# Two chained transformer blocks on one core: three projections token tile by token tile, and one operand stored interleaved

## What is computed

```python
def hybrid_layer(x, c, ...):
    ...
    merged = gates[:, :, 0] * (br_a @ wa) + gates[:, :, 1] * (br_b @ wb) + gates[:, :, 2] * (br_c @ wc)
    y = merged @ w_out
    x = x + gate_m[:, None] * rmsnorm(y, g_mix_post)
    h2 = rmsnorm(x, g_ff_pre) * (1.0 + scale_f[:, None]) + shift_f[:, None]
    y2 = jnp.square(jax.nn.relu(h2 @ w_ff1)) @ w_ff2
    return x + gate_f[:, None] * rmsnorm(y2, g_ff_post)

def second_block(x, mem, ...):
    ...
        x = x + rms_norm(y, post_mix_g[l])
        h = rms_norm(x, pre_x_g[l])
        m = rms_norm(mem, mem_g[l])
        x = x + rms_norm(memory_cross_attention(h, m, w_xq[l], w_xkv[l], w_xo[l]), post_x_g[l])
        h = rms_norm(x, pre_ffn_g[l])
        f = jnp.square(jax.nn.relu(h @ w_ff1[l])) @ w_ff2[l]
        x = x + rms_norm(f, post_ffn_g[l])
```

## Time and profile before

| | us |
|---|---|
| median of 3 runs (lowest, highest) | 831.03 (830.16, 831.48) |
| the profiled execution | 831.31 |
| its span, first to last instruction | 830.1 |
| PE busy | 797.3 |
| DVE, ACT, POOL busy | 566.9, 430.9, 85.6 |
| mean granted TensorE clock | 0.992 |

### The profile page before, as it was taken

How to read it: one execution, slowest core, us unless ns; L and a number is a source line. 1 busy time by engine, 2 the same in 40 slices (tenths; PEclk the granted TensorE clock), 3 DMA queues, 4 the chain that set the end, 5 groups by cost and what they waited for, 6 DMA issues and landing times.

```text
span 830.1 us, 12160 instructions
## 1 busy us (share of the span) xinstructions
PE 797.3 (96%) x4852; PEld 701.6 (85%) x4852; DVE 566.9 (68%) x759; ACT 430.9 (52%) x640; POOL 85.6 (10%) x129
## 2 busy tenths in 40 slices
PE   3999999999989999999999999999999999999995
PEld 2889988999879888888889998788987988888884
DVE  4886987879955575665567889847556566655563
ACT  4445256663446564545456477547545644454441
POOL 6301970001110000000001000011000100000000
PEclk9999999999998999999999999999999999999998
DMA  9978977776644655656656554445434566656641
GB/s 305 363 237 276 356 254 254 280 251 231 227 128 153 195 184 180 195 173 189 200 180 199 176 159 153 151 156 201 154 102 126 156 199 185 196 185 195 183 149 51
DMA packets 83319, 163.64 MB, mean 197 GB/s; under 512 B 5424, under 2 KB 13808, under 8 KB 83264
## 3 DMA queue, kind: packets, MB, share of 16 engines
q1 hardware_dynamic: 81344, 157.31, 58.3%
q10 hardware_dynamic: 1424, 4.81, 1.7%
q0 software_dynamic: 496, 0.76, 0.3%
HBM read 161.81 MB, written 1.05 MB: 196 GB/s over the span
## 4 chain that ended last, share of the span: by engine, by line
PE 83%; DVE 7%; ACT 5%; issue 2%; POOL 1%; DMA 1%; SPq 0%; ACTq 0%; DVEq 0%; POOLq 0%
PE bank L1664 19%; PE bank L1666 18%; PE bank L1665 18%; PE bank L1692 13%; PE bank L1694 6%; DVE ada_acc L924 2%; DVE lo_ring L892 2%; PE bank L1854 1%; ACT hi_ring L472 1%; PE bank L2188 1%; PE bank L2209 1%; DVE x_residual L997 1%; DMA ada_ring<-in_w_ada 1%; PE bank L1723 1%; ACT gates L527 1%
## 5 line engine op out<-in xcount | busy, mean ns | idle before, releaser
L892 DVE TENSOR_TENSOR lo_ring<-raw_ring,hi_ring 128x1024 fp32r<-128x1024 f32 x248 | 306.7, 1240 | 172.6 <-ACT hi_ring L472 172.1
L472 ACT CAST hi_ring<-raw_ring 128x1024 fp32r<-128x1024 f32 x248 | 258.8, 1050 | 272.6 <-PE bank L1666 181.9
L1664 PE MATMUL bank<-h_hi_lo,hi_ring 128*128 128x256 f32 x560 | 164.7, 294 | 4.3 <-DVE lo_ring L892 1.9
L1665 PE MATMUL bank<-h_hi_lo,hi_ring 128*128 128x256 f32 x560 | 159.0, 284 | 0.0
L1666 PE MATMUL bank<-h_hi_lo,lo_ring 128*128 128x256 f32 x560 | 158.9, 284 | 0.0
L1692 PE MATMUL bank<-h_hi_lo,hi_ring 128*128 128x512 f32 x448 | 158.7, 398 | 0.0
L1664 PE MATMUL bank<-hi_ring,branch_hi 128*128 128x512 f32 x320 | 126.6, 395 | 0.0
L1694 PE MATMUL bank<-h_hi_lo,lo_ring 128*128 128x256 f32 x448 | 125.8, 281 | 0.0
L1666 PE MATMUL bank<-hi_ring,branch_lo 128*128 128x512 f32 x320 | 124.8, 390 | 0.0
L1665 PE MATMUL bank<-lo_ring,branch_hi 128*128 128x512 f32 x320 | 124.6, 389 | 0.0
L1664 PEld LDWEIGHTS bank<-h_hi_lo,hi_ring 128*128 128x128 f32 x560 | 108.0, 193 | 9.1 <-issue 4.6
(11 more groups left out here) (269 smaller groups left out, 1036.2 us busy)
## 6 DMA issues: line engine op xcount, KB each, us to landing
raw_ring<-in_w_ff SPq DMA_DIRECT2D x128, 512.0 KB, 4.1
raw_ring<-in_w_in SPq DMA_DIRECT2D x64, 512.0 KB, 4.7
raw_ring<-in_w_out SPq DMA_DIRECT2D x16, 512.0 KB, 3.5
raw_ring<-in_w_xkv SPq DMA_DIRECT2D x16, 512.0 KB, 3.6
mem_v<-in_w_ada SPq DMA_DIRECT2D x12, 512.0 KB, 6.9
ada_ring<-in_w_ada SPq DMA_DIRECT2D x10, 512.0 KB, 5.9
mem_k<-in_w_ada SPq DMA_DIRECT2D x10, 512.0 KB, 5.7
raw_ring<-in_w_branch SPq DMA_DIRECT2D x8, 512.0 KB, 4.8
```

The lines of the kernel that those rows point to most:

```text
L472: act.copy(m.hi[:, m.slot(u)], m.raw[:, m.slot(u)]).then_inc(s.hi_done, 1)
L892: dve.tensor_tensor(m.lo[:, m.slot(u)], m.raw[:, m.slot(u)], as_f32(m.hi[:, m.slot(u)]), ALU.subtract).then_inc(s.lo_done, 1)
L1664: pe.matmul(out, a_hi, b_hi, start=start, stop=False, skip_group_check=True)
L1665: pe.matmul(out, a_hi, b_lo, start=False, stop=False, skip_group_check=True)
```

## The change

In the three places the last four units are passed over twice: first token tile 0 with all four, then token tile 1 with all four (`tile_of`). A new semaphore (`out_tile0`, `post.ahead`) says when tile 0's bank is complete. `used` counts a unit only in the second pass over it. Square sums, gain row, factor and addition go tile by tile in all three (in the first, half n = 0 is still done for both tiles together). POOL's factor is now made of one instruction after the first half's sum (`post_half`) and two (at the end three) after the second's, on one tile (128x1) instead of both (128x2), at all five norms of this kind. `keep_busy` runs between the tiles' transposes, 16 instead of 24 and 6 instead of 12 passes, into bank 0. The output goes out in four pieces of 256 KB, each after its own addition, instead of two of 512 KB. `h_both` is interleaved (hi and lo of each chunk of 128 features side by side), so that L1692 reads 512 columns in one piece; casts and subtractions that write two chunks of it at once now write them as 2x256 (`two` in place of `pair`). The other two norms of this kind keep their order.

Removed lines are shown only where the listing above does not show what they were; `post_square`, `post_scale` and `post_add` are the old ones for one tile.

```diff
...
+BY_HALF = [(n, tt) for n in range(2) for tt in range(NT)]
+BY_TILE = [(n, tt) for tt in range(NT) for n in range(2)]
+    NAMES = ("out_tile0", "out_squares", "out_scaled", "out_rstd", "x_added")
+    def __init__(self, shared, x_parts, order=BY_HALF, ahead=0):
+        self.order = order
+        self.ahead = shared.stage("out_tile0", ahead)
+        self.rstd = shared.stage("out_rstd", NT)
+    def nth(self, n, tt):
+        return self.order.index((n, tt)) + 1
...
+        self.post1, self.post_ff1 = Post(posts, NT, ahead=1), Post(posts, NT)
+        self.post2 = Post(posts, 2 * NT)
+        self.post_x, self.post_ff2 = (Post(posts, 2 * NT, BY_TILE, ahead=2) for _ in range(2))
...
-        self.h_both = sb("h_hi_lo", [2, KD, S], F32R)
-        self.h_hi, self.h_lo = self.h_both[:, 0], self.h_both[:, 1]
+        self.h_both = sb("h_hi_lo", [KD, 2, S], F32R)
+        self.h_hi, self.h_lo = self.h_both[:, :, 0, :], self.h_both[:, :, 1, :]
...
-        sp.wait_ge(*s.post_ff2.x.at(NT + tt + 1))
-        sp.dma_start(out[0][tt * P:tt * P + P, :], m.x[:, tt, :]).then_inc(s.out_done, DMA)
-    sp.wait_ge(s.out_done, NT * DMA)
+        for n in range(2):
+            cs = slice(n * UN, n * UN + UN)
+            sp.wait_ge(*s.post_ff2.x.at(2 * tt + n + 1))
+            sp.dma_start(out[0][tt * P:tt * P + P, cs], m.x[:, tt, cs]).then_inc(s.out_done, DMA)
+    sp.wait_ge(s.out_done, 2 * NT * DMA)
...
+            act.copy(two(m.h_hi, k), two(m.h_f32, k)).then_inc(s.merged_hi, 1)
+    for j in range(RING):
+        if j == RING - 1:
+            post_squares(s.post1, 0, OUT_BANKS[0], OUT + RING)
+        after(OUT + j)
+    act.wait_ge(*s.post1.ahead.at(1))
+    post_square(s.post1, 1, 0, OUT_BANKS[1][0])
+    after(OUT + RING)
+    act.wait_ge(*s.post1.x.at(1))
+    square_sum(s.ff1t, 0, m.x)
+    after(OUT + RING + 1)
+    act.wait_ge(s.used, OUT + 2 * RING)
+    post_square(s.post1, 1, 1, OUT_BANKS[1][1])
+    after(OUT + RING + 2)
+    act.wait_ge(*s.post1.x.at(2))
+    square_sum(s.ff1t, 1, m.x)
+    after(FF1 - 1)
...
+        if post.order is BY_HALF:
+            for q in range(RING):
+                if q % 2:
+                    n = q // 2
+                    post_squares(post, n, (4 + 2 * n, 5 + 2 * n), u + q + 1)
+                after(u + q)
+        else:
+            for n, tt in BY_TILE:
+                if tt == 0:
+                    act.wait_ge(*post.ahead.at(n + 1))
+                else:
+                    act.wait_ge(s.used, u + 2 * n + 2)
+                post_square(post, n, tt, 4 + 2 * n + tt)
...
+    for i in range(XO_AHEAD):
+        after(XO + i)
+    for n in range(2):
+        act.wait_ge(*s.post_x.ahead.at(n + 1))
+        post_square(s.post_x, n, 0, 2 * n)
+    after(XO + XO_AHEAD)
+    after(XO + XO_AHEAD + 1)
+    for n in range(2):
+        act.wait_ge(s.used, FF2 - 1 + n)
+        post_square(s.post_x, n, 1, 2 * n + 1)
+        if n == 0:
+            after(FF2 - 2)
...
+                            dve.tensor_tensor(two(m.h_lo, k), two(m.h_f32, k), as_f32(two(m.h_hi, k)),
+    for j in range(RING):
+        if j == RING - 1:
+            for tt in range(NT):
+                post_scale(s.post1, 0, tt, OUT_BANKS[0][tt], m.rows[:, 0, :])
+        if j == 1:
+            ada_columns(s.ff_cols_ps, s.ff_cols, 6, 8, 24, 32, G_FF)
+        if j == 2:
+            ada_row(s.ff_row_ps, s.ff_rows_in, s.ff_row, m.rows[:, 1, :], 4)
+        after(OUT + j)
+    post_scale(s.post1, 1, 0, OUT_BANKS[1][0], m.rows[:, 0, :])
+    post_add(s.post1, 0, D)
+    after(OUT + RING)
+    scale_rows(s.ff1t, 0, m.x)
+    post_scale(s.post1, 1, 1, OUT_BANKS[1][1], m.rows[:, 0, :])
+    post_add(s.post1, 1, D)
+    after(OUT + RING + 1)
+    after(OUT + RING + 2)
+    scale_rows(s.ff1t, 1, m.x)
+    after(FF1 - 1)
...
+        if post.order is BY_HALF:
+            for q in range(RING):
+                if q % 2:
+                    n = q // 2
+                    for tt in range(NT):
+                        post_scale(post, n, tt, 4 + 2 * n + tt, row)
+                after(u + q)
+            for tt in range(NT):
+                post_add(post, tt, width)
+        else:
+            for tt in range(NT):
+                for n in range(2):
+                    post_scale(post, n, tt, 4 + 2 * n + tt, row)
+                post_add(post, tt, width)
...
+    for i in range(XO_AHEAD):
+        after(XO + i)
+    for tt in range(NT):
+        for n in range(2):
+            post_scale(s.post_x, n, tt, 2 * n + tt, m.rows[:, 1, :])
+            if tt == 1 and n == 0:
+                after(FF2 - 2)
+        post_add(s.post_x, tt, UN)
+        if tt == 0:
+            after(XO + XO_AHEAD)
+            after(XO + XO_AHEAD + 1)
...
+    def norm_tile(turn, tt):
+        pool.wait_ge(*turn.squares.at(tt + 1))
+        ins = rstd(stat[:, tt:tt + 1], stat[:, 2 + tt:3 + tt], stat[:, 4 + tt:5 + tt], D)
+        ins.then_inc(turn.rstd.sem, 1)
+        pool.wait_ge(*turn.rstd.at(tt + 1))
+            norm_tile(turn, tt)
+    def post_half(post, tt, c=1.0 / D):
+        pool.wait_ge(*post.squares.at(post.nth(0, tt)))
+        own.then(pool.tensor_scalar(stat[:, 24 + tt:25 + tt], stat[:, 20 + 2 * tt:21 + 2 * tt], c, EPS, ALU.mult,
+                                    ALU.add))
+    def post_rstd(post, tt, c=1.0 / D, factor=None):
+        pool.wait_ge(*post.squares.at(post.nth(1, tt)))
+        dst = stat[:, 28 + tt:29 + tt]
+        own.then(pool.tensor_scalar(stat[:, 26 + tt:27 + tt], stat[:, 21 + 2 * tt:22 + 2 * tt], c,
+                                    stat[:, 24 + tt:25 + tt], ALU.mult, ALU.add))
+        ins = pool.tensor_tensor(dst, stat[:, 26 + tt:27 + tt], m.half[:, 0:1], ALU.pow)
+        if factor is not None:
+            ins = pool.tensor_tensor(dst, dst, factor, ALU.mult)
+        pool.wait_ge(*post.rstd.at(tt + 1))
+    def post_rstds(post):
+        for tt in range(NT):
+            post_half(post, tt)
+        for tt in range(NT):
+            post_rstd(post, tt)
...
+    for tt in range(NT):
+        post_half(s.post1, tt)
+    for tt in range(NT):
+        post_rstd(s.post1, tt)
+        norm_tile(s.ff1t, tt)
+    post_rstds(s.post_ff1)
...
+    post_rstds(s.post2)
+    for tt in range(NT):
+        post_half(s.post_x, tt)
+        post_rstd(s.post_x, tt)
+    own.then(pool.tensor_scalar(m.r4, m.r4, 1.0 / D, 1.0, ALU.mult, ALU.mult))
+    for tt in range(NT):
+        post_half(s.post_ff2, tt, m.r4[:, tt:tt + 1])
+        post_rstd(s.post_ff2, tt, m.r4[:, tt:tt + 1], m.r2[:, tt:tt + 1])
...
-                pe.matmul(b.rearrange("p (a s) -> p a s", a=2), m.hi[:, slot, k, fc], x_both[:, :, k0 + k, :],
+                pe.matmul(b, m.hi[:, slot, k, fc], x_both[:, k0 + k].rearrange("p a s -> p (a s)"),
-                mm = pe.matmul(b[:, 0:S], m.lo[:, slot, k, fc], x_both[:, 0, k0 + k, :], start=False,
+                mm = pe.matmul(b[:, 0:S], m.lo[:, slot, k, fc], x_both[:, k0 + k, 0, :], start=False,
-    def unit_tokens(u, k0, x_hi, x_lo, outs, first, last, cols=slice(0, UN), start_first=True, beside=None):
+    def unit_tokens(u, k0, x_hi, x_lo, outs, first, last, cols=slice(0, UN), start_first=True, beside=None,
+                    tiles=range(NT)):
-            for tt in range(NT):
+            for tt in tiles:
...
+    def tile_of(tt, u, k0, x_hi, x_lo, b0, first, last):
+        return unit_tokens(u, k0, x_hi, x_lo, (bank[b0][:, :], bank[b0 + 1][:, :]), (first,) * NT, (last,) * NT,
+                           tiles=(tt,))
...
     def keep_busy(n):
+        if n:
+            claim(0)
         for _ in range(n):
-            pe.matmul(bank[7][:, :], m.h_hi[:, 0, 0:P], pair(m.h_hi, 0), start=True, stop=True)
+            pe.matmul(bank[0][:, :], m.h_hi[:, 0, 0:P], m.h_both[:, 0].rearrange("p a s -> p (a s)"), start=True, stop=True)
     def turn_normed(turn, idle=0):
-        keep_busy(idle)
+            if tt:
+                keep_busy(idle)
     def turn_x(turn, post, idle=0):
-        keep_busy(idle)
-        for n in range(2):
-            for tt in range(NT):
-                pe.wait_ge(*post.x.at(n * NT + tt + 1))
+        for tt in range(NT):
+            if tt:
+                keep_busy(idle)
+            for n in range(2):
+                pe.wait_ge(*post.x.at(2 * tt + n + 1))
...
+    claim(*OUT_BANKS[0])
+    for j in range(RING):
+        pe.wait_ge(s.merged_lo, j + 1)
+        tokens(OUT + j, UK * j, m.h_hi, m.h_lo, OUT_BANKS[0][0], j == 0, j == RING - 1, beside=ff_cols if j == 0 else None)
+        if j == 1:
+            pe.wait_ge(s.ada_used, ADA_UNITS)
+            ada_row(2, 4).then_inc(s.ff_row_ps, 1)
+            free[4], free[5] = (s.ff_row, 1), (s.ff_row, 3)
+    claim(*OUT_BANKS[1])
+    for tt in range(NT):
+            mm = tile_of(tt, OUT + RING + j, UK * j, m.h_hi, m.h_lo, OUT_BANKS[1][0], j == 0, j == RING - 1)
+            if tt == 1:
+                mm.then_inc(s.used, 1)
+            elif j == RING - 1:
+                mm.then_inc(s.post1.ahead.sem, 1)
```

(28 more changed lines are left out.)

139 lines of the change are left out of this document (26 added, 113 removed).

## The result

The changed kernel is **faster: a median of 824.88 us** over 5 runs (822.05 to 825.80), against 831.03 (828.88 to 831.62) of before in the same session. The ratio is 0.993 (95% interval 0.9912 to 0.9949), some 5.8 us: 0.7%, small, but the interval excludes 1. The forecast was 823.1 with a range up to 825.0. By the ratio the time is 831.03 x 0.993 = 825.2, just outside the range; the raw median lies just inside. Either way the sign was right and the forecast gain 2 us too large. Among the runs of the experiments two executions, one of before and one of full_before, ran at a granted clock of 0.65 (1127 and 1144 us), and the ratios leave them out.

A forecast was written before the change was run, and what follows sets the result against it. PE was busy 797.3 of 830.1 us, so gains lay in three waits where the chain leaves it: 2.9 + 1.1 + 3.9 = 7.9 us, giving 823.1 against the median 831.03; range 819.0 to 825.0.

The forecast's parts named there:

- Before FF1: Wait between the last `w_out` pass and the first feed-forward's first feature pass: 2.9 us gained, first feature at 247.3.
- POOL's small step at 0.21: In the norm before FF1: POOL's small instruction 0.21 us, power 0.55, with steps between them 0.9 per tile.
- That the clock falls once more and that the feature passes pay for it as before.: Before FF1, PE has little to do from 243.2 to 247.3, so half clock returns at the old cost.
- My bound for a worse fall: Before FF1: the clock falls a little later and stays low while features run, costing 0.3 us more than before.
- Before FF2: Wait between the last `w_xo` pass and the second feed-forward's first feature pass: 1.1 us gained, clock staying up.
- DVE's list and not POOL ends the wait: Before FF2: DVE reaches the addition at 637.75, POOL is ready at 637.25; without DVE in the way, gain 1.5.
- The end: After PE's last pass, through norm and stores: 3.9 us gained, bounds 3.0 and 4.2, end at 826.1.
- the 2.2 that I chose: At the end: the last 256 KB store lands 2.2 us after issue, with half as much data in flight.
- estimate of 2.6 us for 256 KB: At the end: store time by the skill's fixed part and rate; with it the gain would be 3.5 us.
- Interleaving: Two-part source of the 512-column passes made contiguous: costed at nothing, bounds 0 and 4 us.
- the clock stays up: Rival before FF1: no fall of the clock, 1.5 us more gained, 821.6 us; chance 0.17.
- PE did not starve: Rival where units are passed twice: PE waits for units in the first pass, 833 us if so; chance 0.02.

The follow-up runs named there:

- full_before: The kernel before, with idle passes added through the waits before both feed-forwards: medians 829.48 us (ratio 0.9992) and, run again, 828.94 (0.9980).
- 825.86: Profiled execution, 825.86 us, of the unaltered changed kernel run again; its clock falls before FF1. Those six runs: median 825.87, ratio 0.9931 to before.
- low_a: Changed kernel with the last but one unit's low part before FF1 moved behind tile 1's row scaling: 822.30 us, ratio 0.9905 to before.
- no_idle: Changed kernel without its 16 idle passes between the two tiles' transposes before FF1: 825.87 us, ratio 0.9941 to before.
- low_b: Changed kernel with one unit's cast and low part before FF2 moved behind the last squares and additions: 822.28 us, ratio 0.9905 to before.
- full_two_parts: Changed kernel with added idle passes before both feed-forwards, less the interleaving of high and low parts: 822.98 us, ratio 0.9905 to before.
- full_no_first: Changed kernel with added idle passes before both feed-forwards, less the new order before FF1 (POOL's factors by tile stay): 823.51 us, ratio 0.9915.

## Why the forecast was 2 us too low

Against before, with the fall of the clock in both (825.86 against 831.31 as profiled), the spans differ by 5.6 us, and by 5.8 with the 0.2 later start taken off: before FF1 1.0 (a gap shorter by 2.25 less the 1.25 that the way behind it is longer), before FF2 1.0, at the end 3.85. The forecast had 7.9.

**Before FF1: 2.9 forecast, 1.0 measured. This is where it failed,** in three steps.
- The gap is 9.95 and not 9.3, a gain of 2.25. I took POOL's small step at 0.21 "and steps between them 0.9"; it lasts 0.98 beside DVE's low parts. I had moved low parts next to it on DVE's list, noted their price for DVE and not for POOL. low_a: removed, the gap is 9.2, the forecast's to 0.1. Before had a sign of it that I hadn't looked at: its own POOL step for tile 1, beside the row scaling, took 0.48 us (at 244.85) where tile 0's took 0.19 (at 243.67).
- "That the clock falls once more and that the feature passes pay for it as before." The first half held in most runs, the second never: the half clock ended where it had (253.7, 253.5), the features came 2.0 us earlier, and 5.4 us of them ran at half clock in place of 3.3. That takes back 0.9 (2.4 less 1.46), and no_idle shows the same proportion on a third overlap. My bound for a worse fall was 0.3.
- The 0.3 us inside FF1, which I had not seen coming and which stays unexplained.

Together they are 0.65 + 0.9 + 0.3, the 1.9 us between forecast and measured gain here.

**Before FF2: 1.1 forecast, 1.0 measured**, for half the wrong reason. "DVE's list and not POOL ends the wait": it was POOL, stretched from 0.27 to 0.87 by a low part; without it (0.6) and without the cast in front of the last square sum (0.25) low_b gains 0.9 more. The clock stayed up, as forecast.

**The end: 3.9 forecast, 3.85 measured.** Factor 2.2 us after the last pass instead of 1.9 to 2.0, last addition 3.7 instead of 3.5, and the stores made it up: 2.0 us in place of the 2.2 that I chose. The sum came out right here by errors that cancel, and the 2.2 was a choice. Its base was short too: 3.0 us is the median of two stores that fly together, and the last one of before took 3.3. The prediction's estimate of 2.6 us for 256 KB by the Trainium skill ("DMA: Bandwidth & Descriptors", "Anatomy of one DMA — SWDGE (gpsimd) path") was further off on this queue.

**Interleaving: nothing forecast, nothing measured.** L1692's successor kept its mean and full_two_parts its time.

Of the rivals, "the clock stays up" was given 1.5 us; it happens from run to run and is worth 2.4 now, so the median depends on how often. PE did not starve but for 0.05 us: in `w_out` the fourth unit, to which I had given 0.2 us to spare, held a pass up at 231.30 (825.86). From FF1's transposes to the gap before FF2 it is 332.93 us before and 332.92 now, from FF2's first feature to the last pass 178.23 in both. The range ended 1.9 us above the forecast, and the worse fall was in it with 0.3. With that fall at 0.9, the 0.65 of POOL's step and the 0.3 inside FF1 the sum would have been 825.0, in the place of the 825.2 measured.

## What to carry to other kernels

A stretch of half clock is a thing of its own in the timeline: when work behind it moves ahead, ask how much of it now runs inside, and fill the wait with passes that compute nothing until no run shows a fall; here that was worth 2.4 us in each run that fell, more than either of the change's first two places, and the larger part of the scatter. The 1.0 to 1.4 us from the start of the program stays. When large VectorE instructions are moved between the steps of a chain, look at GpSimd's small steps in that chain too: this cost 0.8 us before FF1 and 0.6 before FF2. And compare instants of the trace, gap by gap, where runs scatter by more than what is looked for.

## What the runs showed that was not expected

- A GpSimd multiply-add on 128x1 took 0.19 us with VectorE idle, 0.27 beside the gain row (one input from PSUM, one from SBUF), 0.48 beside the row scaling, and 0.87 to 0.98 while VectorE subtracted 128x1024 from SBUF and to SBUF; it ended 0.06 and 0.13 us behind VectorE's instruction. Beside an addition of 128x1024 its power step took 1.50 us instead of 0.57 (full_no_first, 240.27).
- Alternating passes of 512 and 256 columns cost 5 ns a pair over running them in two groups (2.3 us over 448).
- The fall before FF1 cost 0.43 to 0.45 us for each microsecond of feature passes inside it.
- The program has two starts, 1.0 to 1.4 us apart, by when TensorE's clock first comes up.
- A store of 256 KB landed in 2.0 us, one of 512 KB in 2.6 alone and in 3.3 as the second of two together.
